# PEER expert output: 512 dense prompt columns on TensorE, the 32 sample columns from gathered expert rows

## What is computed

```python
def block(xb):                      # xb: 128 tokens x 2048
    qh = einsum('td,de->te', xb, w_pq).reshape(128, 8, 2, 128)
    s = einsum('thcd,hckd->thck', qh, sub_keys)
    sv, si = top_k(s, 16)           # per half: 16 of 128 keys
    cand = sv[:, :, 0, :, None] + sv[:, :, 1, None, :]
    cid = si[:, :, 0, :, None] * 128 + si[:, :, 1, None, :]
    top_s, top_pos = top_k(cand.reshape(128, 8, -1), 16)
    eid = take_along_axis(cid.reshape(128, 8, -1), top_pos, axis=-1)
    gate = softmax(top_s)
    act = gelu(einsum('thkd,td->thk', u_experts[eid], xb))
    return einsum('thk,thkd->td', gate * act, v_experts[eid])
```

## Time and profile before

| | us |
|---|---|
| median of 3 runs (5111.02 to 5119.5) | 5116.29 |
| the profiled execution | 5119.69 |
| its span in the trace | 5117.5 |
| output stage, first matmul with `chi` to the last | 3547 to 5088 |
| PE busy, of the span | 5005.5 (98%) |
| DVE, ACT, POOL busy | 2452.4, 1231.9, 1206.5 |

### The profile page before, as it was taken

How to read it: one execution, slowest core, us unless ns; L and a number is a source line. 1 busy time by engine, 2 the same in 40 slices (tenths; PEclk the granted TensorE clock), 3 DMA queues, 4 the chain that set the end, 5 groups by cost and what they waited for, 6 DMA issues and landing times. The chain is left out here.

```text
span 5117.5 us, 92582 instructions
## 1 busy us (share of the span) xinstructions
PE 5005.5 (98%) x39028; PEld 4930.2 (96%) x39028; DVE 2452.4 (48%) x3709; ACT 1231.9 (24%) x1251; POOL 1206.5 (24%) x522
## 2 busy tenths in 40 slices
PE   8999999999989999999999999999999999999997
PEld 8999888899969999999999999999999999999997
DVE  4455556533222335765777776501444444444443
ACT  4233334222121222222111111122212212212212
POOL 0000000020001003333333333334223233233232
PEclk9999999899989999999999999999999999999998
DMA  3233433232342234333444344443333333333332
GB/s 150 96 130 119 153 105 108 93 121 90 132 149 86 95 108 164 120 120 106 137 132 150 133 153 137 153 165 144 135 138 128 135 135 129 138 131 129 141 125 76
DMA packets 233944, 651.28 MB, mean 127 GB/s; under 512 B 13696, under 2 KB 126720, under 8 KB 177024
## 3 DMA queue, kind: packets, MB, share of 16 engines
q1 hardware_dynamic: 233856, 650.03, 36.0%
HBM read 539.42 MB, written 110.56 MB: 127 GB/s over the span
## 5 line engine op out<-in xcount | busy, mean ns | idle before, releaser
L237 PE MATMUL pu<-xhi,whi 128*128 128x272 f32 x7456 | 1548.0, 289 | 28.6 <-DVE xlo L503 12.5
L237 PE MATMUL pu<-xhi,wlo 128*128 128x272 f32 x7456 | 1545.9, 289 | 0.0
L237 PE MATMUL pu<-xlo,whi 128*128 128x272 f32 x7456 | 1540.7, 288 | 0.0
L237 PEld LDWEIGHTS pu<-xhi,whi 128*128 128x128 f32 x7456 | 1174.4, 189 | 31.5 <-issue 24.3
L237 PEld LDWEIGHTS pu<-xlo,whi 128*128 128x128 f32 x7456 | 1175.2, 189 | 0.0
L237 PEld LDWEIGHTS pu<-xhi,wlo 128*128 128x128 f32 x7456 | 1167.2, 189 | 0.0
L221 ACT CAST whi<-raw 128x2048 fp32r<-128x2048 f32 x393 | 748.5, 1905 | 1593.3 <-PE pm L237 1183.5
L226 POOL TENSOR_TENSOR wlo<-raw,whi 128x2048 fp32r<-128x2048 f32 x128 | 601.5, 4699 | 1210.1 <-ACT whi L221 1210.1
L226 DVE TENSOR_TENSOR wlo<-raw,whi 128x2048 fp32r<-128x2048 f32 x265 | 609.4, 2300 | 390.9 <-ACT whi L221 383.9
L1492 POOL TENSOR_TENSOR clo<-coef,chi 128x544 fp32r<-128x544 f32 x124 | 261.6, 2130 | 994.3 <-ACT chi L1496 994.3
L1556 DVE TENSOR_TENSOR x<-pm,x 128x544 f32<-128x544 f32 x256 | 185.5, 724 | 584.1 <-PE pm L237 584.1
(11 more groups left out here) (298 smaller groups left out, 4796.4 us busy)
## 6 DMA issues: line engine op xcount, KB each, us to landing
raw<-units SPq DMA_DIRECT2D x393, 1024.0 KB, 4.9
h_s<-h_out SPq DMA_DIRECT2D x128, 272.0 KB, 2.1
gate_s<-table SPq DMA_DIRECT2D x17, 2048.0 KB, 9.4
h_in<-h_s SPq DMA_DIRECT2D x32, 1088.0 KB, 7.1
gate_in<-gate_s SPq DMA_DIRECT2D x32, 1088.0 KB, 9.1
q_s<-q_out SPq DMA_DIRECT2D x32, 320.0 KB, 2.2
x<-xT SPq DMA_DIRECT2D x8, 1088.0 KB, 6.7
qh<-q_s SPq DMA_DIRECT2D x8, 1088.0 KB, 7.3
```

Of the source, the lines that this page charges most:

```text
L237: ins = nc.tensor.matmul(out, w, xs[b][m == 1], start=(first and n == 0 and m == 0), stop=(last and n == len(terms) - 1 and m == 2))
```

## The change

The output stage leaves out the 32 sample columns: its operands have 512 columns, one matmul takes all of them into one PSUM bank, and a group has 192 matmuls in place of 384. `coef`, `chi`, `clo`, `h_in`, `gate_in`, `gate_s` and the adds to `x` have 512 columns, and the table of gates has 16 chunks. The hidden stage still computes all 544 columns.

The sample columns come from the chosen experts' rows. The fifth block of queries holds the 32 sample tokens four times over; so each of four 32-partition parts keeps two of the eight heads: 32 *slots* per partition, 128 x 32 = 4096 chosen experts. For a slot POOL issues one indirect DMA for 128 hidden values out of `h_s` and 16 for 128 expert rows out of `units` (128 pieces of 512 bytes each), into one of three `rows` buffers. Two groups later DVE multiplies the hidden values by the gates and adds `rows` times that to `row_sum` (128 x 2048). Ahead of the last pair PE sums `row_sum` over the four parts with a 0/1 matrix, and DVE adds that to the sample columns of `x`. `slots_of` gives groups 0, 6, 12, 18 and 24 two slots, the other groups up to 26 one, and the last five none. The loops of DVE and POOL over the pairs are written out.

```diff
-    gate_s = nc.dram_tensor("gate_s", (NGRP, P, T * GRP), F32, kind="Internal").ap()
+    gate_s = nc.dram_tensor("gate_s", (NGRP, P, TP * GRP), F32, kind="Internal").ap()
...
+                    if experts:
+                        again = lambda ap: ap.unsqueeze(1).broadcast_to([P, 3, TS])
+                        nc.vector.tensor_tensor(q_out[:, s, T:TPAD].rearrange("p (c n) -> p c n", n=TS), again(pu[:, slot, 1, TP - HALF:HALF]),
+                                                again(rinv[:, TP:T]), ALU.mult)
...
-    TCH = T // TC
+    TCH = TP // TC
...
+    def dve_keep_slots(chain):
...
+        for g in range(P // TS):
+            ps, cs = slice(TS * g, TS * (g + 1)), slice(SLOTS * g, SLOTS * (g + 1))
+            v.tensor_copy(row[ps], flat(row_key)[ps, cs])
+            v.tensor_copy(col[ps], flat(col_key)[ps, cs])
+            ins = v.tensor_copy(slot_gate[ps], flat(gate)[ps, cs])
...
-        with pe.Fori(0, NCH) as t:
+        with pe.Fori(0, NCH - 1) as t:
+            stretch(t, True)
+        stretch(NCH - 1, False)
...
+    rows = [place(f"rows{i}", [KT, P]) for i in range(3)]
+    row_sum = place("row_sum", [KT, P])
+    slots_of = lambda group: range(min(group + (group + 5) // 6, SLOTS), min(group + 1 + (group + 6) // 6, SLOTS)) if group >= 0 else ()
+
+    def pool_rows(pool, group):
+        for j in slots_of(group):
+            s = j % 3
+            if j >= 3:
+                pool.wait_ge(row_used, j - 2)
+            nc.gpsimd.indirect_dma_start(slot_h[:, j:j + 1], None, h_s.rearrange("k p (t o) -> (k p t) o", o=1),
+                                         bass.IndirectOffsetOnAxis(ap=slot_at[:, j:j + 1], axis=0)).then_inc(row_loaded[s], 16)
+            for o in range(KT):
+                nc.gpsimd.indirect_dma_start(rows[s][:, o], None, a["units"].rearrange("u p (t n) -> (u p t) n", n=P),
+                                             bass.IndirectOffsetOnAxis(ap=slot_row[:, j:j + 1], axis=0),
+                                             element_offset=o // 4 * (P * KT * P) + o % 4 * (GRP * P)).then_inc(row_loaded[s], 16)
+
+    def dve_row(dve, j):
+        s = j % 3
+        dve.wait_ge(row_loaded[s], 16 * (KT + 1) * (j // 3 + 1))
+        nc.vector.tensor_tensor(slot_h[:, j:j + 1], slot_h[:, j:j + 1], slot_gate[:, j:j + 1], ALU.mult).then_inc(slots_kept, 1)
...
+            ins = nc.vector.scalar_tensor_tensor(row_sum[:], rows[s][:], slot_h[:, j:j + 1], row_sum[:], ALU.mult, ALU.add)
+        ins.then_inc(row_used, 1)
+
+    def pe_sample(pe):
+        pe.wait_ge(row_used, SLOTS)
+        for k in range(KT):
+            ins = nc.tensor.matmul(pm[:, 0, 1, k * TS:(k + 1) * TS], row_sum[:, k], consts[:, C_SEL:C_SEL + TS], start=True, stop=True)
+        ins.then_inc(sample_out, 1)
...
-                    products([out_slot(d)[:, b, 0:HALF] for b in (0, 1)],
-                             [(whi[:, slot, GRP * d + k], wlo[:, slot, GRP * d + k], halves(chi[r], clo[r], k)) for k in range(GRP)],
+                    products([out_slot(d)[:, 0, 0:TP]],
+                             [(whi[:, slot, GRP * d + k], wlo[:, slot, GRP * d + k], [(chi[r][:, k], clo[r][:, k])]) for k in range(GRP)],
...
         for n in range(2 * VU):
+            if n % 2 == 0:
+                for j in slots_of(2 * i + n // VU - 2)[n % VU // 2:n % VU // 2 + 1]:
+                    dve_row(dve, j)
+            if last and n == 1:
+                dve_sample(dve)
...
-                nc.vector.tensor_tensor(in_two(x[:, o]), out_slot(d)[:, :, 0:HALF], in_two(x[:, o]), ALU.add).then_inc(psum_free, 1)
+                nc.vector.tensor_tensor(x[:, o, 0:TP], out_slot(d)[:, 0, 0:TP], x[:, o, 0:TP], ALU.add).then_inc(psum_free, 1)
...
         pool_coefs(pool, i * 2 + 1, 1, i + 1)
+        pool_rows(pool, 2 * i)
         if not last:
             pool_coefs(pool, i * 2 + 2, 0, i + 2)
+            pool_rows(pool, 2 * i + 1)
...
+        with pe.Fori(0, NGRP // 2 - 1) as i:
+            pair_pe(pe, i)
+        pe_sample(pe)
+        pair_pe(pe, NGRP // 2 - 1)
...
+        pool.wait_ge(slots_kept, 1)
+        finished(pool, V0)
+        for s in (0, 1):
+            pool.wait_ge(h_stored[s], 8 * P + PRIME)
```

More of the change, by code:

```diff
@@ L77 @@
 C_VALID = C_CNT + 64
-NC = C_VALID + NCH * HEADS
+C_SEL = C_VALID + NCH * HEADS
+C_TOK = C_SEL + TS
+NC = C_TOK + 1
 def constants():
@@ L96, in constants @@
     v[TS:, NCH - 1] = 0.0
-    c[:, C_VALID:NC] = v.reshape(P, -1)
+    c[:, C_VALID:C_SEL] = v.reshape(P, -1)
+    c[:, C_SEL:C_TOK] = r[:, None] % TS == r[None, :TS]
+    c[:, C_TOK] = TP + r % TS
     return c
@@ L961, in projected @@
                         taken(sp, u)
-                        sp.wait_ge(pad_cleared, run + 1)
+                        if not experts:
+                            sp.wait_ge(pad_cleared, run + 1)
                         sp.dma_start(q_s[bass.ds(2 * i + s, 1)].rearrange("k p n -> (k p) n"), q_out[:, s]).then_inc(q_stored[s], 16)
@@ L1140, in _ @@
                     split.pool(pool)
-                nc.gpsimd.memset(q_out[:, :, T:TPAD], 0.0).then_inc(pad_cleared, 1)
+                if not experts:
+                    nc.gpsimd.memset(q_out[:, :, T:TPAD], 0.0).then_inc(pad_cleared, 1)
                 with pool.Fori(0, KT // 2) as i:
@@ L1194, in build @@
     place = region(WR + 8 * T, W_SIZE - 8 * T)
-    h_in = [place(f"h_in{i}", [GRP, T]) for i in (0, 1)]
-    gate_in = [place(f"gate_in{i}", [T, GRP]) for i in (0, 1)]
-    coef = place("coef", [GRP, T])
+    h_in = [place(f"h_in{i}", [GRP, TP]) for i in (0, 1)]
+    gate_in = [place(f"gate_in{i}", [TP, GRP]) for i in (0, 1)]
+    coef = place("coef", [GRP, TP])
+    SLOTS = 8 * TOPK // (P // TS)
+    slot_gate, slot_h = gcol[:, 0:SLOTS], beta[:, 0:SLOTS]
+    slot_row, slot_at = (t[:, 0:SLOTS].bitcast(U32) for t in (gcum, egcum))
+    row_loaded = [sem(f"row_loaded{i}") for i in range(3)]
+    row_used = sem("row_used")
+    sample_out = sem("sample_out")
+    slots_kept = sem("slots_kept")
     keys_loaded = sem("keys_loaded")
@@ L1262, in pe_turn, with dve_route @@
         ins.then_inc(slots_turned, 1)
-    def dve_route(dve, t, chain):
+    def dve_keep_slots(chain):
+        link, v = chain.link, nc.vector
+        flat = lambda t: t[:].rearrange("p h k -> p (h k)")
+        part = lambda t, n: flat(t)[:, n * SLOTS:(n + 1) * SLOTS]
+        row, col, expert, scaled_expert = (part(fa, n) for n in range(4))
+        tile, row_at, h_at = (part(fb, n) for n in range(3))
+        row_int, tile_int = part(ia, 0), part(ib, 0)
+        for g in range(P // TS):
[3 more added lines that the diff above has]
+            ins = v.tensor_copy(slot_gate[ps], flat(gate)[ps, cs])
+        link(ins)
+        link(v.tensor_copy(row_int, row))
+        link(v.tensor_scalar(tile_int, row_int, GRP - 1, None, ALU.bitwise_and))
+        link(v.tensor_copy(tile, tile_int))
+        link(v.scalar_tensor_tensor(expert, row, float(P), col, ALU.mult, ALU.add))
+        link(v.tensor_scalar(scaled_expert, expert, float(KT), float(V0 * P * KT), ALU.mult, ALU.add))
+        link(v.scalar_tensor_tensor(row_at, tile, float(1 - P * KT), scaled_expert, ALU.mult, ALU.add))
+        link(v.scalar_tensor_tensor(h_at, expert, float(T), consts[:, C_TOK:C_TOK + 1].broadcast_to([P, SLOTS]), ALU.mult, ALU.add))
+        v.tensor_copy(slot_row, row_at)
+        v.tensor_copy(slot_at, h_at).then_inc(slots_kept, 1)
+    def dve_route(dve, t, chain, sample=False):
         link = chain.link
@@ L1313, in dve_route @@
         link(v.reciprocal(rs[:], sm[:]))
-        v.tensor_tensor(gate[:], ex[:], rs[:].unsqueeze(2).broadcast_to([P, 8, TOPK]), ALU.mult).then_inc(slots_ready, 1)
+        share = v.tensor_tensor(gate[:], ex[:], rs[:].unsqueeze(2).broadcast_to([P, 8, TOPK]), ALU.mult)
+        if sample:
+            link(share)
+            dve_keep_slots(chain)
+            return
+        share.then_inc(slots_ready, 1)
         dve.wait_ge(slots_turned, t + 1)
@@ L1424, in hidden_stage_tensor, with stretch @@
     def hidden_stage_tensor(pe):
-        with pe.Fori(0, NCH) as t:
+        def stretch(t, turned):
             def between(m, n):
@@ L1430, in between @@
                     pe_scores(pe, t)
-                if (m, n) == (STRETCH - 1, KT - 2):
+                if turned and (m, n) == (STRETCH - 1, KT - 2):
                     pe_turn(pe, t)
@@ L1460, in hidden_stage_vector @@
     def hidden_stage_vector(dve):
-        with dve.Fori(0, NCH) as t:
-            chain = Chain(dve, route_chain)
+        chain = Chain(dve, route_chain)
+        with dve.Fori(0, NCH - 1) as t:
             chain.enter(t, ROUTE_LINKS)
@@ L1465, in hidden_stage_vector @@
             assert chain.n == ROUTE_LINKS, chain.n
-        dve.wait_ge(slots_taken, NCH + PRIME)
+        chain.enter(NCH - 1, ROUTE_LINKS)
+        dve_route(dve, NCH - 1, chain, sample=True)
+        dve.wait_ge(slots_kept, 1)
+        dve.wait_ge(slots_taken, NCH - 1 + PRIME)
         dve.wait_ge(x_parked, 16)
@@ L1470, in hidden_stage_vector @@
```

(38 more changed lines are left out.)

5 lines of the change are left out of this document (2 added, 3 removed).

## The result

The changed kernel takes **5076.29 us** (median of 4 runs, 5073.93 to 5079.46) beside 5114.31 us for the kernel before. The ratio is 0.9925 with a 95% interval of 0.9908 to 0.9942: faster by 0.75%, 38 us. The forecast was 4991 us, a gain of 125 us. The direction and the range hold; under a third of the gain arrived.

What follows compares the result with a forecast made beforehand. PE, busy 98% of the span, was taken as the bound: 5119.7 − 132.1 (wider matmuls) − 0.2 (small PE terms) + 3.4 (POOL stalls) = 4990.8, forecast 4991 us, range 4962 to 5095.

Steps and rivals of the forecast that it cites:

- The gain on PE: Output stage: 12288 matmuls of 272 columns, 1538.5 us, become 6144 of 512 columns, 1406.4 us; gain 132.1 us.
- The other small edits: On PE: one table chunk less, −3.8 us; three transposes fewer, under half a us, left out.
- The tail: Time behind PE's last matmul, claimed to stay unchanged.
- X: Time one gather occupies POOL: taken as 1.2 us, between bounds of 0.36 and 1.9.
- the prediction's formula for the two-slot groups: Five groups with 34 gathers: above X = 1.18 us each stalls 34 × (X − 1.18); +3.4 us in all.
- what costs nothing, and its cover: DVE's row, landing waits, SP loads, gathered traffic, routing and the copied queries' multiplication were all claimed hidden, adding no time.
- 4 us of cover: DVE's split after the row ends 6.8 us into the unit; its product is wanted at 10.99.
- Rival 2: Slower: POOL's issue becomes the bound at `pool_rows`, from X = 1.72 us; 5216 us at X = 1.9; chance 0.14.
- Rival 1: POOL often late, gain partly eaten: X 1.45 to 1.69, +46 to +114 us, 5033 to 5101; chance 0.17.
- the forecast's own case: X up to 1.45 with either matmul distance: 4962 to 5033 us, chance 0.62.
- Rival 3: Output stage: a wide matmul is no cheaper than two narrow ones, 0.25 us; 5123 us, no change; chance 0.03.
- three signs of being wrong: Gathers start over 1.48 us apart, `coef` comes late in every group, or DVE waits at `row_loaded`.

Runs made afterwards that it cites:

- the two kernels whose PE does not wait: Changed kernel with `pool_rows` not called and `row_sum` zeroed: 4969.15 us; changed kernel with `coef` moved ahead of the gathers, nothing left out: 4973.1 us.
- `coef` first: Against the changed kernel, POOL's `coef` for the group after next moved ahead of the gathers, behind the last `clo`: 4973.1 us, 0.9721 of the kernel before.

## Why the prediction was wrong

**The gain on PE was right, and larger than taken.** The forecast had 0.2289 us from start to start, 1406 us; measured is 0.227. Without waits the time was to be 4987; the two kernels whose PE does not wait take 4969 and 4973. `pe_sample` was put at 3.6 us and takes 3.5. The other small edits show no wait in the stage. The tail, from the last start of the stage to the end of the span, was to stay and is 32.0 us in place of 29.6; the cause was not looked for.

**Mis-sized: X, the time of one gather on POOL.** The forecast took 1.2 us. A gather by itself takes 0.94 and 0.30 to the next, 1.25 from start to start; one that meets DVE's split takes 2 to 3 us. The 512 row gathers and the gaps ahead of them sum to 570.3 + 156.0 us, 1.42 each; the 34 of group 0 take from 3561.18 to 3608.32, 1.39 each. By the prediction's formula for the two-slot groups, 34 × (1.39 − 1.18) = 7 us for each, 36 in all where 3 were put down. The form of that step held: the large waits stand in exactly the five groups it named, at the unit it named.

**The step that failed: "what costs nothing, and its cover".** It took DVE's split as 2.29 us and DVE's row as 2.3 us wherever they stood, with 4 us of cover. Rival 2 did weigh the contention of the two engines, but one way only, with DVE holding POOL. The other way was not priced, although the change moves POOL's two-input instructions onto DVE's. It is now seen in three places:

- in the large waits the split takes 7.49 − 2.29 = 5.2 us longer; with 7 us of lateness that gives 12.2, measured 12.6 in four of the five and 14.0 in the first;
- at the head of a group the row's first instruction takes 4.7 us in the median. With the row and the split behind it, the split of group 3 ends 10.1 us into the unit where 6.8 were put down, the 4 us of cover are used up, and the waits of 23.7 us before the second units follow;
- behind the waits the clock falls for some us, most of the 16.6 us in the table above.

36 + 26 + 24 + 17 + 3.5 is some 106 of the 108 us. So the cover of the second unit was right; what DVE does within it was mis-sized.

**The rivals.** Rival 1, POOL late and the gain partly eaten, has the right outcome: 5076 lies inside its 5033 to 5101. But it starts at X = 1.45, and X came out at 1.39 to 1.42, within the forecast's own case. With 1.42 the prediction's formula gives 170 × (1.42 − 1.18) = 41 us of stalls and 5028 us; the 48 us from there to 5076, and the 12 that PE gained more, are DVE's hold and the slower clock, which no rival had. So it is luck that the time lies inside this rival and inside the range. Rival 2 did not come: X stayed below 1.72, and with `coef` first even 34 gathers are hidden. Its supposition that a gather is held by DVE's split is right. Rival 3 is refuted by the kernel without gathers. None of the three signs of being wrong appeared: gathers start 1.42 us apart on average, `coef` is late for ACT in five groups only (and at the stage's start), and DVE never waits at `row_loaded`. But PE waited in 18 groups that the prediction had not named, and that was the sign of the hold.

**What was overlooked** is a question of order. The prediction counted that `coef` waits behind 34 or 17 gathers, and asked only whether it was late for ACT. It did not ask what else runs at the time to which `coef` was moved. What stays open is why DVE gets no turn between two instructions of POOL's run; the traces show only that it does not.

## What to carry to other kernels

When slow work is put into an engine's idle time, put it behind what the other engines wait for next, not ahead of it: here that order alone was worth 103 us. When work of one engine moves in time, lay its new interval over the other engines' rows, and where a trace shows one engine holding another, price the hold both ways. Here a two-input VectorE instruction that started during a run of two-input GpSimd instructions was held to the end of that run, and one that started 1 us ahead of the run was not held.

## What the runs showed of the hardware

- **GpSimd holds VectorE over a whole run of instructions.** A VectorE instruction on one number per partition, 0.15 us alone, took up to 7.17 us and ended when GpSimd's back-to-back two-input instructions did. One of these takes some 1.5 us, so it was held for more than the rest of one. DVE's timeline in the changed kernel, then POOL's:

```profile
3647.19 7.17 DVE L1555 TENSOR_TENSOR beta<-beta,gcol 128x1 f32<-128x1 f32 x1
```

```profile
3645.78 6.08 POOL L1425 TENSOR_TENSOR coef<-h_in,gate_in 128x512 f32<-128x512 f32 x4
3651.80 2.53 POOL L1584 TENSOR_TENSOR clo<-coef,chi 128x512 fp32r<-128x512 f32 x2
```

- **A gather on GpSimd is held by a two-input VectorE instruction.** The gather that starts within the split below takes 2.68 us, its neighbours 0.94. The Trainium skill's page "SBUF — State Buffer", section "Who interferes with whom", infers that making descriptors is not blocked by such an instruction. The trace shows the gather as a whole held; but a gather also reads its 128 addresses from a tile (`gcum`), and no run separates the two, so that inference is neither borne out nor refuted here. POOL's timeline in the changed kernel, then DVE's:

```profile
3566.38 0.94 POOL L1548 DMA_INDIRECT rows<-units,gcum  x1 [0.30 <-issue]
3567.63 2.68 POOL L1548 DMA_INDIRECT rows<-units,gcum  x1 [0.30 <-issue]
```

```profile
3567.20 2.29 DVE L230 TENSOR_TENSOR wlo<-raw,whi 128x2048 fp32r<-128x2048 f32 x1 [1.25 <-ACT whi L225]
```

- **A wait of PE can cost more than itself.** After the 14 us wait the granted clock was 0.53 over 3622 to 3627, near the lower of the two levels of 1.2 and 2.4 GHz, and matmuls started 0.43 us apart for about 4 us. After the 2.9 us wait of group 8 it was 0.61 over 3941 to 3945, with starts 0.43 apart for 3 us. After the waits of 0.5 to 1.9 us of this kernel no such stretch is seen. The window behind the 14 us wait:

```profile
3622.00:3627.00 5.00, 4.46 (x11) 3.54 (x12) 3.88 (x4) 0.00 (x0) 4.09 (x3) 0.53 0.61 223
```
